# Raw fp32 weights for the small expert jobs, on two column halves of the array, and expert blocks of 1,792 columns

## The reference

```python
def swiglu(x, w_gate, w_up, w_down):
    return (jax.nn.silu(x @ w_gate) * (x @ w_up)) @ w_down

def moe_swiglu(x, w_router, w_gate, w_up, w_down):
    logits = (x @ w_router).astype(jnp.float32)
    top_vals, top_idx = lax.top_k(logits, TOP_K)        # 2 of 8
    top_w = jax.nn.softmax(top_vals, axis=-1)
    gates = jnp.sum(jax.nn.one_hot(top_idx, N_EXPERTS) * top_w[..., None], axis=-2)
    out = jnp.zeros_like(x)
    for e in range(N_EXPERTS):                          # gate, up 1024 x 3584; down 3584 x 1024
        out = out + gates[..., e:e + 1] * swiglu(x, w_gate[e], w_up[e], w_down[e])
    return out
```

## Time and profile before

| | us |
|---|---|
| median of 3 runs | 1379.75 (1378.05 to 1380.9) |
| profiled execution | 1377.29 |
| its span | 1375.6 |
| PE busy | 1324.6 (96%) |
| DVE busy | 1144.9 (83%) |
| ACT busy | 988.4 (72%) |

### The profile page before, as it was taken

One profiled execution on the slowest core, in us unless ns is written; L12 is line 12 of the kernel. 1 busy time (PEld: TensorE's weight loads), 2 busy tenths in 40 slices (PEclk: granted clock), 3 DMA queues, 4 the chain that ended last, 5 costly groups with the idle time before them and its releaser, 6 DMA issues.

```text
span 1375.6 us, 19519 instructions
## 1 busy us (share of the span) xinstructions
PE 1324.6 (96%) x6863; PEld 1138.8 (83%) x6863; DVE 1144.9 (83%) x1048; ACT 988.4 (72%) x954; POOL 129.6 (9%) x119
## 2 busy tenths in 40 slices
PE   9999999999999999999999999999999999999987
PEld 8978888888997888878878888878888887787865
DVE  5767544467665999999999999999999999899986
ACT  5555433456555787888878888887888888787884
POOL 2000000000000097900000000000000002000000
PEclk9999999999999999999999999999999999999999
DMA  9955555567443799999999999999999999999980
GB/s 321 262 182 187 184 186 193 190 215 233 169 139 107 273 403 410 412 408 411 398 406 413 409 411 413 400 411 407 408 412 410 401 413 408 411 408 399 406 348 31
DMA packets 135622, 447.36 MB, mean 325 GB/s; under 512 B 8441, under 2 KB 30085, under 8 KB 123278
## 3 DMA queue, kind: packets, MB, share of 16 engines
q1 hardware_dynamic: 130592, 430.99, 81.8%
q0 software_dynamic: 3072, 8.91, 1.9%
q10 hardware_dynamic: 1902, 6.71, 1.5%
HBM read 438.04 MB, written 8.54 MB: 325 GB/s over the span
## 4 chain that ended last, share of the span: by engine, by line
PE 57%; DMA 17%; DVE 13%; issue 7%; ACT 4%; SPq 1%; ACTq 0%; DVEq 0%
PE banks L1265 16%; PE banks L1845 15%; DVE w_lo L2068 9%; DMA raw<-in_o_exp_gate 8%; DMA raw<-in_o_exp_down 7%; PE banks L1299 5%; PE banks L1866 4%; PE banks L1604 4%; PE banks L1918 4%; ACT w_hi L720 3%; PE banks L1882 1%; DMA raw<-in_e_w_in 1%; PE banks L1829 1%; SPq L405 1%; DMA raw<-in_o_exp_up 1%
## 5 line engine op out<-in xcount | busy, mean ns | idle before, releaser
L2068 DVE TENSOR_TENSOR w_lo<-raw,w_hi 128x1792 fp32r<-128x1792 f32 (+1 forms) x454 | 918.5, 2064 | 114.6 <-PE banks L1265 49.9
L720 ACT ACTIVATE w_hi<-raw 128x1792 fp32r<-128x1792 f32 (+1 forms) x454 | 784.6, 1737 | 265.4 <-PE banks L1265 79.7
L1866 PE MATMUL banks<-w_lo,x_hi 128*128 128x448 f32 x512 | 130.8, 377 | 15.8 <-DVE w_lo L2068 15.1
L1845 PE MATMUL banks<-w_hi,x_hi 128*128 128x448 f32 x512 | 128.0, 372 | 0.0
L1866 PE MATMUL banks<-w_hi,x_hi 128*128 128x448 f32 x512 | 125.8, 368 | 0.3 <-ACT w_hi L720 0.2
L1845 PE MATMUL banks<-w_lo,x_hi 128*128 128x448 f32 x512 | 125.7, 367 | 0.2 <-DVE w_lo L2068 0.2
L1866 PEld LDWEIGHTS banks<-w_lo,x_hi 128*128 128x128 f32 x512 | 91.8, 188 | 40.8 <-DVE w_lo L2068 34.7
L1845 PE MATMUL banks<-w_hi,x_lo 128*128 128x448 f32 x512 | 125.3, 366 | 0.0
L1265 PE MATMUL banks<-w_hi,x_lo 128*128 128x512 f32 (+1 forms) x304 | 108.5, 357 | 0.3 <-DVE x_lo L2103 0.3
L1265 PE MATMUL banks<-w_lo,x_hi 128*128 128x512 f32 (+1 forms) x304 | 108.1, 356 | 0.0
L1265 PE MATMUL banks<-w_hi,x_hi 128*128 128x512 f32 (+1 forms) x304 | 108.1, 356 | 0.0
(11 more groups left out here) (349 smaller groups left out, 1834.4 us busy)
## 6 DMA issues: line engine op xcount, KB each, us to landing
raw<-in_o_exp_gate SPq DMA_DIRECT2D x128, 896.0 KB, 8.0
raw<-in_o_exp_up SPq DMA_DIRECT2D x128, 896.0 KB, 8.8
raw<-in_o_exp_down SPq DMA_DIRECT2D x96, 1024.0 KB, 9.6
raw<-in_o_exp_down SPq DMA_DIRECT2D x32, 512.0 KB, 7.4
raw<-in_o_w_qkv SPq DMA_DIRECT2D x12, 1024.0 KB, 6.5
raw<-in_e_ffn_gate SPq DMA_DIRECT2D x11, 1024.0 KB, 5.2
raw<-in_e_ffn_up SPq DMA_DIRECT2D x11, 1024.0 KB, 5.5
raw<-in_e_ffn_down SPq DMA_DIRECT2D x11, 1024.0 KB, 4.9
```

The costliest lines, as they stand in the source:

```text
L720: act.activation(w_hi[:, at % HI, 0:size], raw[:, at % RAW, 0:size], ACT.Copy).then_inc(hi_made, 1)
L1845: mm = pe.matmul(bank[first + f][:, 0:CUT // 2], x[:, 2 * k + kk, 0:P], w[:, kk, f * (CUT // 2):(f + 1) * (CUT // 2)], start=start and kk ...
L1866: mm = pe.matmul(bank[first + f][:, 0:CUT // 2], x_two[:, 2 * k + kk, :], w[:, kk, f * (CUT // 2):(f + 1) * (CUT // 2)], start=start and k ...
L2068: ve.tensor_tensor(w_lo[:, at % LO, 0:size], raw[:, at % RAW, 0:size], w_hi[:, at % HI, 0:size], ALU.subtract)\
```

## The change

An expert is now done in 2 blocks of 1,792 columns, each of two sides of 896. A superstep has 48 tiles (it equals two old blocks), and only the 24 wide ones are split. A gate or up tile is one chunk of 128 contraction rows by 1,792 columns, so one row of 7,168 B on each partition. The order within a superstep: 8 wide gates, 2 small downs of the block before, 8 wide ups, 6 small downs, 8 small gates, 8 small ups, 8 wide downs.

A small tile is multiplied as it landed: the array takes the raw fp32 tile as moving operand and the 64 rows of `x_small` (not split) as stationary one, side 0 on the array's columns 0 to 63 and side 1 on columns 64 to 127. The results of both sides lie in the two halves of the partitions of one bank, complete, so nothing is folded. For a small down the two halves are the two halves of the output. The slot of a small tile is freed by PE (`tile_used`), that of a wide one by DVE (`lo_made`). Wide gates, wide ups, small gates and small ups share banks 0 to 3; the small result has bank 4, gathered rows are turned in bank 5. Some buffers share memory that had their own (`r_raw`, `conv_w`, `zeros_r`, `rrow`). In layer 0, two splits on ACT move behind the copies of the attention's keys and values, and the copy of the values comes before that of the keys. In the opening the gated projection's first product is finished ahead of the gather, and all 16 wide gate and up tiles precede the first small one.

The core of the diff:

```diff
-BLOCKS = D_FFE // CUT
+SIDES = 2
+UP = SIDES * CUT
+BLOCKS = D_FFE // UP
...
-STEP_TILES = 24
+STEP_TILES = 48
+WIDE_TILES = STEP_TILES // 2
+WIDE_GATE, WIDE_UP, SMALL_GATE, SMALL_UP, WIDE_DOWN = 0, 10, 24, 32, 40
+SMALL_DOWN = (8, 9, 18, 19, 20, 21, 22, 23)
...  SP
+            def load_at(i, cols, src, j, b, closing=False):
+                was = wide_no(i - RAW, b is None, closing)   # None: the tile six earlier was small
+                if was is None:
+                    sp.wait_ge(tile_used, tile_at(i - RAW, j, b) + 1)
+                else:
+                    sp.wait_ge(lo_made, wide_at(was, j, b) + 1)
+                slot = (MOE_T - SKIP + i) % RAW
...
-            for k in range(4):
-                up(eg, first_small, 0, k, 12 + k, None, None)
...  ACT, layer 0
-            split(Q0_T + 1 + HI)
             act.wait_ge(tile_used, KV_T + 1)
+            act.activation(v0T, bank[4][:, SEQ:2 * SEQ], ACT.Copy).then_inc(kv0_made, 1)
             act.activation(k0T, bank[4][:, 0:SEQ], ACT.Copy).then_inc(kv0_made, 1)
-            act.activation(v0T, bank[4][:, SEQ:2 * SEQ], ACT.Copy).then_inc(kv0_made, 1)
-            split(KV_T + HI)
...
+            split(Q0_T + 1 + HI)
+            split(KV_T + HI)
...  PE
             def small_up(first, k, i, j, b):
-                wait_high(tile_at(i, j, b))
-                product(hi, start=k == 0)
-                wait_tile(tile_at(i, j, b))
-                product(lo, stop=k == 3).then_inc(tile_used, 1)
+                slot = wait_loaded(i, j, b)
+                for f in range(2):
+                    for s in range(SIDES):
+                        at = s * CUT + f * (CUT // 2)
+                        mm = pe.matmul(bank[first + f][s * SMALL:(s + 1) * SMALL, 0:CUT // 2], x_small[:, k, :],
+                                       raw[:, slot, at:at + CUT // 2], start=k == 0, stop=k == KC - 1, skip_group_check=True)
+                mm.then_inc(tile_used, 1)
...
             def small_down(k, i, j, b, start=False, stop=False):
+                slot = wait_loaded(i, j, b)
+                for kk, (s, q) in enumerate(chunks_of(k)):
+                    for half in range(2):
+                        at = kk * D + half * HALF
+                        mm = pe.matmul(bank[4][half * SMALL:(half + 1) * SMALL, :], hidT_s[:, q, s, :], raw[:, slot, at:at + HALF],
+                                       start=start and (k, kk) == (0, 0), stop=stop and k == DOWNS - 1, skip_group_check=True)
+                mm.then_inc(tile_used, 1)
...
+            def superstep(j, b, first=False, placing=False):
+                for k in range(KC):
+                    wide_up(k, k, j, b)
+                for k in range(2):
+                    small_down(k, SMALL_DOWN[k], j, b, start=not first)
+                pe.wait_ge(e_silu_made, SIDES * step_no(j, b))
+                for k in range(KC):
+                    wide_up(k, KC + k, j, b)
+                for k in range(2, 5):
+                    small_down(k, SMALL_DOWN[k], j, b)
+                turn_wide(j, b)
...
+                second_half(j, b, turn_next=not first and not placing, starting=first, stopping=not first)
```

More of the change, by code:

```diff
@@ new lines, in superstep @@
+            def superstep(wide, of, small_was, of_was, small, j, b):
+                for k in range(KC):
+                    up(eg, wide, of, k, WIDE_GATE + k, j, b)
+                for k in range(2):
+                    down(small_was, of_was, k, SMALL_DOWN[k], j, b)
+                for k in range(KC):
+                    up(eu, wide, of, k, WIDE_UP + k, j, b)
+                for k in range(2, DOWNS):
+                    down(small_was, of_was, k, SMALL_DOWN[k], j, b)
+                second_half(wide, small, of, j, b)
@@ L509, in small_of @@
                 return sp.value_load(job_int[0:1, bass.ds(j + MOST, 1)], min_val=0, max_val=EXPERTS - 1)
-            def blocks(wide, small, j, count=BLOCKS - 1):
-                with sp.Fori(1, count + 1) as b:
-                    superstep(wide, b, small, b + (-1), small, j, b)
-            for k in range(4):
-                up(eg, 0, 0, k, 4 + k, None, None)
-            for k in range(4):
-                if k == 2:
+            for k in range(KC):
+                if k == 6:
                     for t in range(TT):
@@ L1875, in wide_down @@
[L1875 to L1894 removed]
+                wait_tile(wide_at(w, j, b))
@@ new lines, in wide_down, with product @@
+            def wide_down(k, j, b, start=False, stop=False):
+                w = 16 + k
+                hi, lo = [t.rearrange("p (c n) -> p c n", n=D) for t in (w_hi[:, (MOE_T + w) % HI], w_lo[:, (MOE_T + w) % LO])]
+                def product(half, hidden, weights, begin=False, end=False):
+                    for kk, (s, q) in enumerate(chunks_of(k)):
+                        mm = pe.matmul(bank[6 + half], hidden[:, s * PARTS + q, :], weights[:, kk, half * HALF:(half + 1) * HALF],
+                                       start=begin and kk == 0, stop=end, skip_group_check=True)
+                    return mm
+                wait_high(wide_at(w, j, b))
+                for half in range(2):
+                    product(half, hidT_hi, hi, begin=start and k == 0)
+                if k == DOWNS - 1 and stop:
+                    wait_tile(wide_at(w, j, b))
@@ L2042, in _ @@
-            small_down(1, 1, last, BLOCKS)
-            pe.wait_ge(place_made, 1)
+                superstep(j, 1)
+                superstep(j, BLOCKS, first=True)
+            superstep(last, 1, placing=True)
+            for k in range(6):
+                small_down(k, k, last, BLOCKS)
             scatter_wide(last)
-            small_down(2, 2, last, BLOCKS)
-            small_down(3, 3, last, BLOCKS, last=True)
+            for k in range(6, DOWNS):
+                small_down(k, k, last, BLOCKS, stop=True)
@@ L2238, in _ @@
             split(KV_T)
-            for i in range(3):
+            for i in range(2):
                 split(LO + i)
@@ L2616, in block @@
-                lo(23, j, b, final)
+                for w in range(20, 24):
+                    lo(w, j, b)
             split(OUT1_T + 2 + LO)
```

823 lines of the change are left out of this document (319 added, 504 removed).

## The result

The changed kernel takes 1426.96 us (median of 4 runs, 1423.57 to 1429.45) against 1379.57; the recorded ratio is 1.0351 [1.0334, 1.0368], so 47 us slower by the medians and 48 by the ratio. The forecast was 1373, faster than before, with a range up to 1402: wrong in sign. The profiled execution has a span of 1426.1 us.

What follows compares the result with a forecast made beforehand. DMA was taken as the floor, with PE close behind. Opening, supersteps and end -13.5, layer 0 -0.6, clock +7.2: -6.9 from 1379.75 gives 1373 us; range 1354 to 1402, the forecast's own 1364 to 1386.

Steps and rivals of the forecast that it cites:

- Prices of tiles: Expert stage: 7,168 B row 274 ns, small up 1.50 us with halves together, DMA 107.1 us a superstep.
- What is late next: the ring of six: Expert supersteps: slots released late after the wide run give a period of 108.7 us; 7 periods, -7.7 us.
- DMA so stands dry for 1.6 us a superstep: Right after the wide ups: DMA idle 1.6 us a superstep, leaving 1.1 of the 2.7 us the rows save.
- The chain's first term: Start of wide downs: from landing of the first tile, ACT's and DVE's splits and last product end at 5.4 us.
- that I put at nothing: Sign of a wrong forecast: a PE wait, as for gathered rows or small hidden values, showing in every superstep.
- Where neither engine ends last: DVE and ACT in the expert stage: load falls to about half, which alone brings nothing.
- Opening: Before the first superstep's small tiles: table wait hides, 16 wide tiles run first; first wide down landed at 522.4 us.
- End: Eighth wide down run to last projection: 47 us (45 to 49), projection at 1330.3 instead of 1343.83, -13.5.
- Clock: PE's idle before wide downs: six clock falls at eight places, 1.2 us each, +7.2 us.
- Nowhere else: Sign: stretches at 0.5 of the clock only at the start of the wide downs.
- Rival 3: Clock falls inside the small run, PE falls behind DMA and releases slots late: 1398 us; chance 0.17.
- Waits in the chain: Bound on the forecast for waits in the superstep's chain: -9 to +9 us.

Runs made afterwards that it cites:

- buf: Changed kernel plus late's two moved copies; ACT also copies small tiles into the ring of high parts, low parts left out: 1383.6 us, ratio 1.0046 to before.
- late: Changed kernel with ACT's copies of the turned small values and of the gathered rows' second half moved later: 1415.8 us, ratio 1.0257 to before.
- before_ring: Kernel before, but the load queue waits for PE's use instead of DVE's split where the tile six places earlier was small: 1405.74 us, ratio 1.0197.

## Why the prediction was wrong

- **Prices of tiles.** Right: 274 ns a row, 1.51 us a small up, halves at the same time, 107.4 us of transfer a superstep for 107.1. At the change from the full array to column halves about 0.1 us goes: the last wide up starts its last four products at 707.18 and the small downs start 0.91 us later, where 0.81 (a third of 2.44) is the pace. The Trainium skill (TensorEngine Tiling (Array Packing), Key Properties) says that changing the tiling mode drains TensorE. The trace is in line with that; the products also change to raw fp32 there, so the 0.1 us isn't shown to be the drain's.
- **What is late next: the ring of six.** This step failed. It put a period at 108.7 us; it was 116.4, which in seven periods is 54 us, the size of the whole miss (the falls of the clock, which the forecast counted apart, are in it). "DMA so stands dry for 1.6 us a superstep" at one place, 11 us in seven; there, in the small downs behind the ups, it lost 13.1, nearly as forecast, but 48.6 us elsewhere. The step followed one chain from the wide downs to the seventh small tile and took the loads as ready wherever that chain didn't touch them. It counted six slots as 13 us of lead, and not that the change takes from small tiles the three places further that the second buffer gave them. (The chain's first term, put at 5.4, adds up to 5.1 from its parts, and the period before to 109.9; neither matters here.) The step knew what frees a slot ("only now is a slot released") and used it at one place of the superstep alone. The forecast came near the second cause itself, among waits of PE "that I put at nothing", those for the small hidden values; the wait is ACT's, for PE to turn them, 3.4 us at a time, and with the gathered rows' copy it is 13 us of the kernel.
- **Where neither engine ends last.** "As neither ends last now, this alone brings nothing": DVE and ACT were not the bound, but their splits emptied the ring. Taking half of them away cost the ring its outlet for small tiles; buf has ACT copy them again and gains 29 us over late.
- **Opening.** Right within 2 us: the first wide down's tile lands at 524.4, forecast at 522.4, and PE starts on it at 526.4.
- **End.** Put at 47 us, from the landing of the last run of wide downs to the projection; from 1339.19 to 1391.95 it is 52.8, as PE waits 5.54 us for DVE, which splits two tiles before it adds rows.
- **Clock.** Seven falls at the eight places, where six were forecast, and the size was nearly right as well: 6 us back where 7.2 were put. "Nowhere else" was wrong: the clock also fell behind both jumps back, for 10 us at the last projection, and once inside a small run, the last, behind an idle of 1.98 us (a mean of 0.76 from 1313 to 1320 us, against 1.00 from 610 to 635). Rival 3 needed this in every superstep; once in eight small runs, it isn't the cause.
- **Jumps.** Not thought of: 13 us, or 11 by the medians.
- **The bounds.** "Waits in the chain (-9 to +9)" is the term that should have held this. It was taken around a sum in which loads wait for PE at one place only.

The gains over the changed kernel, in steps of the ratio: late 0.9%, copies into the second ring 2.1%, end 0.8%, jumps 0.5% behind the second ring (1.0% without it). Together 4.3%, the way from 1.0351 to 0.9921; they add up because each kernel contains the edits of the one before it, and in another order the shares could differ.

## What to carry to other kernels

When a step between landing and use is removed, ask what its buffers did: here a split that was no bound let loads run up to three tiles further ahead of the engine that uses them, and taking it away turned a kernel bound by DMA into one that waits on its landing ring. Count for each tile when its slot is free again, by whom, and what stands ahead of that in the engine's order; and count DMA by bytes against the price of its packets, since its busy share can read 1.0 while less is moved (1.01 at 396 GB/s in before_ring, 1.02 at 408 before).

## What the runs showed that I had not expected

- A jump back over a loop body of two supersteps (about 790 products of PE, counted from the code) lasts 6.0 and 5.9 us on PE, by the branch records of the changed kernel, and holds up the load queue for 5.1 and 5.2 us until its next instruction. In the kernel before, whose bodies hold about 250 (inner loop) and 500 products, no jump takes more than 0.35 us on any engine. Written out, the loop has no such stop. That the length of the body is the reason isn't shown.
- A packet takes longer the fewer loads are under way (issued by SP and not yet landed). A row of 7,168 B in the changed kernel, from 530 to 1340 us, takes 336 ns on average with one load under way, 326 with two, 300 with three, 287 with four, 278 with five and 277 with six.
- Two idles of PE of the same length before the same product, 2.70 us in front of 875.01 and 989.22 us, have a fall of the clock behind the one and none behind the other; the rows of the four microseconds from there (the clock is the third number from the right):

```profile
875.00:879.00 4.00, 3.98 (x11) 3.18 (x12) 3.74 (x2) 2.88 (x2) 0.00 (x0) 0.58 1.02 424
989.00:993.00 4.00, 3.56 (x14) 2.66 (x15) 3.54 (x2) 2.86 (x3) 0.00 (x0) 1.00 1.01 420
```
